# Score products behind the transposes in the dense and the banded attention loops

## The reference

```python
# first block, each layer: swiglu; then a mixer of three branches; then swiglu
y_a = fourier_mix(a_in) @ w_br_a[l]
y_b = dilated_mixture(qb, kb, vb, rel_bias[:, :DIL_HEADS]) @ w_br_b[l]
y_c = diff_attention(qc, kc, vc, ...) @ w_br_c[l]      # the dense loop
merged = gates[:, :, 0] * y_a + gates[:, :, 1] * y_b + gates[:, :, 2] * y_c
# diff_attention: 4 heads, 4 blocks of 128 queries, 512 keys, two maps m
p = jax.nn.softmax(logits, axis=-1)
a = p[:, :, 0] - lam * p[:, :, 1]
o = jnp.einsum('bhqk,bkhe->bqhe', a, vf)
# second block: banded attention with a sink, a gated delta net, cross attention, swiglu
attn_o = _window_attention(aq, ak, av, attn_sink[l])    # the banded loop: keys within 128
```

## Time and profile before

| | before |
|---|---|
| median of three runs | 3817.81 us |
| the profiled execution | 3812.61 us |
| its span | 3810.5 us |
| TensorE products busy | 3582.8 us, 94% |
| TensorE weight loads busy | 2932.3 us, 77% |
| VectorE busy | 1588.3 us, 42% |
| ScalarE busy | 1353.9 us, 36% |
| GpSimd busy | 1480.5 us, 39% |

### The profile page before, as it was taken

How to read it: one execution, slowest core, us unless ns; L and a number is a source line. 1 busy time by engine, 2 the same in 40 slices (tenths; PEclk the granted TensorE clock), 3 DMA queues, 4 the chain that set the end, 5 groups by cost and what they waited for, 6 DMA issues and landing times.

```text
span 3810.5 us, 50432 instructions
## 1 busy us (share of the span) xinstructions
PE 3582.8 (94%) x16768; PEld 2932.3 (77%) x16768; DVE 1588.3 (42%) x2199; ACT 1353.9 (36%) x2332; POOL 1480.5 (39%) x1124
## 2 busy tenths in 40 slices
PE   8999998999999999999989999998888978779997
PEld 6888886778888788878767888886668867558886
DVE  4223225644322422232265442324876675333224
ACT  4224222644322433242346342324571013233223
POOL 4445430345444544454213544443220006225443
PEclk9999998999999999999999999999898989989999
DMA  3223310122222322232112322222110003112222
GB/s 116 94 99 104 117 67 32 63 98 94 95 98 95 105 99 94 99 128 87 46 43 72 105 94 99 94 99 89 50 61 1 1 17 121 50 44 96 97 97 91
DMA packets 86868, 309.59 MB, mean 81 GB/s; under 512 B 9775, under 2 KB 11825, under 8 KB 86244
## 3 DMA queue, kind: packets, MB, share of 16 engines
q1 hardware_dynamic: 82512, 297.96, 23.1%
q10 hardware_dynamic: 4244, 10.14, 1.0%
HBM read 305.89 MB, written 2.17 MB: 81 GB/s over the span
## 4 chain that ended last, share of the span: by engine, by line
PE 89%; DVE 6%; ACT 2%; issue 2%; ACTq 0%; POOL 0%; DMA 0%; DVEq 0%; POOLq 0%
PE ps L416 25%; PE ps L418 25%; PE ps L417 25%; PE ps L814 1%; PE ps L822 1%; PE ps L818 1%; PE ps L563 1%; PE ps L586 1%; PE ps L473 1%; PE ps L453 1%; PE ps L475 1%; PE ps L576 1%; PE ps L501 0%; PE ps L728 0%; PE ps L881 0%
## 5 line engine op out<-in xcount | busy, mean ns | idle before, releaser
L381 POOL TENSOR_TENSOR w_lo<-raw,w_hi 128x512 fp32r<-128x512 f32 x1120 | 1480.3, 1328 | 2301.5 <-ACT w_hi L911 1825.9
L416 PE MATMUL ps<-u_hi,w_hi 128*128 128x512 f32 (+1 forms) x2990 | 1178.3, 394 | 34.2 <-DVE u_lo L1643 16.9
L418 PE MATMUL ps<-u_lo,w_hi 128*128 128x512 f32 (+1 forms) x2990 | 1160.1, 388 | 0.0
L417 PE MATMUL ps<-u_hi,w_lo 128*128 128x512 f32 (+1 forms) x2990 | 1159.8, 388 | 0.0
L416 PEld LDWEIGHTS ps<-u_hi,w_hi 128*128 128x128 f32 x2990 | 569.4, 190 | 165.6 <-issue 41.9
L417 PEld LDWEIGHTS ps<-u_hi,w_lo 128*128 128x128 f32 x2990 | 569.0, 190 | 116.2 <-issue 5.2
L418 PEld LDWEIGHTS ps<-u_lo,w_hi 128*128 128x128 f32 x2990 | 567.8, 190 | 114.7
L913 ACT ACTIVATE w_hi<-raw 128x512 fp32r<-128x512 f32 x560 | 352.5, 629 | 766.5 <-PE ps L418 765.8
L416 PE MATMUL ps<-m_hi,w_hi 128*128 128x512 f32 x1344 | 532.7, 396 | 17.3 <-DVE m_lo L1408 11.9
L911 ACT ACTIVATE w_hi<-raw 128x512 fp32r<-128x512 f32 x560 | 350.9, 627 | 519.6 <-PE ps L418 484.2
L417 PE MATMUL ps<-m_hi,w_lo 128*128 128x512 f32 x1344 | 527.4, 392 | 0.0
(11 more groups left out here) (389 smaller groups left out, 2823.6 us busy)
## 6 DMA issues: line engine op xcount, KB each, us to landing
raw<-jobs SPq DMA_DIRECT2D x560, 512.0 KB, 3.2
tab<-vec_dram ACTq DMA_DIRECT2D x8, 448.0 KB, 5.1
tab<-dft_in ACTq DMA_DIRECT2D x2, 1156.0 KB, 5.2
x<-x_in SPq DMA_DIRECT2D x4, 512.0 KB, 6.5
out<-x SPq DMA_DIRECT2D x8, 256.0 KB, 2.0
tab<-chunk_in ACTq DMA_DIRECT2D x1, 1024.0 KB, 4.8
tab<-mem_in ACTq DMA_DIRECT2D x1, 1024.0 KB, 4.9
tab<-vec_dram ACTq DMA_DIRECT2D x4, 128.0 KB, 7.7
```

The source lines that it names most:

```text
L381: pool.tensor_tensor(w_lo[:, s, w], raw[:, s, w], w_hi[:, s, w].bitcast(F32), ALU.subtract).then_inc(lo_done[s], 1)
L416: pe.matmul(ps[bank][:, 0:n], w_hi[:, s, w], hi[:, k, 0:n], start=k == ks[0], stop=False)
L417: pe.matmul(ps[bank][:, 0:n], w_lo[:, s, w], hi[:, k, 0:n], start=False, stop=False)
L418: last = pe.matmul(ps[bank][:, 0:n], w_hi[:, s, w], lo[:, k, 0:n], start=False, stop=k == ks[-1])
```

## The change

In both loops the call of `scores(u + 2)` moves from the head of the round to the place behind the transposes, ahead of the job. Nothing else is changed.

```diff
@@ dense
                 for u in range(16):
-                    if u < 14:
-                        scores(u + 2)
                     h = 3 - u // 4
                     pe.wait_ge(prob_done, c.next("prob"))
                     pe.wait_ge(tr_copied, c.take("tr_copied"))
                     for k in range(4):
                         mm = pe.transpose(ps[4][:, k * P:k * P + P], T[:, 2 * (u % 2) + 1, k * P:k * P + P], ident)
                     mm.then_inc(tr_full, c.up("tr_full"))
+                    if u < 14:
+                        scores(u + 2)
                     if u % 2 == 0:
                         job(0, u_hi, u_lo)
```

## The result

| | before | after |
|---|---|---|
| median of 7 runs each, same chip | 3817.81 us | 3830.08 us |
| lowest and highest | 3814.16, 3820.9 | 3825.04, 3831.78 |
| the profiled execution | 3812.61 us | 3825.04 us |
| its span | 3810.5 us | 3822.9 us |
| mean granted clock of it | 0.966 | 0.964 |

The ratio is 1.0031, with a 95% interval from 1.0019 to 1.0042: the change costs 12.3 us (7.3 to 16.0 by that interval), more than the 0.2% that a measurement can tell. The forecast of 3818.8 us and its range up to 3824.5 were too low.

What follows compares the result with a forecast made beforehand. TensorE was taken as the bound, with 89% of the chain that ended last. Steady rounds -1.2, dense starts +2.3 and banded start -0.1 summed to +1.0 us, for a median of 3818.8 us, range 3813.0 to 3824.5.

Steps and rivals of the forecast that it cites:

- Steady rounds: 13 rounds in each loop, 39 in all: -0.03 us a round, -1.2 us together, between -5.1 and +3.5.
- Transposes to scores: New pair of starts on TensorE in each steady round, taken as 0.45 us between 0.35 and 0.57.
- First to second product: Start of the job behind the scores in each steady round: 0.33 us, where it was 0.31.
- values to transposes: New pair of starts in each steady round: 0.89 us, read from the last rounds, which have no scores.
- scores to job: New pair of starts in each steady round: 1.06 us, the same as scores to transposes had before.
- Starts: Round 2's scores lose their cover at the dense loop's start, run twice: +2.3 us, between +2.2 and +4.2.
- The banded start: Start of the banded loop, once: transposes go first, job starts earlier; -0.1 us, between -0.3 and +0.1.
- The sum over the loops: Steady rounds plus dense and banded starts: +1.0 us, between -3.2 and +7.8.
- rows 7 and 8: Profile rows of the first dense loop's start: TensorE at 1.2 GHz, clock rise behind 662.2; 1.15 us lost a time.
- A new wait for the probabilities: Rival at the transposes of even rounds: late probabilities cost 12.6 us on top of the 1.0, 3831.4 us; chance 0.07.
- Loads pulled ahead: Rival: the job's first load hides behind the scores, 0.19 us saved in each of 39 rounds, 3811.4 us; chance 0.05.
- Nothing at all: Rival: the edit has no effect, starts not exposed because the clock rises earlier by as much, 3817.8 us; chance 0.08.

Runs made afterwards that it cites:

- banded only: New order in the banded loop alone, dense loops as in the kernel before the change: 3818.84 us against 3806.99, ratio 1.0024.
- rounds 1 to 13 alone: New order in rounds 1 to 13 of each loop, round 0 as before: 3822.90 us against 3806.99; repeated, 3824.07 against 3817.66.

## Why the prediction was wrong

*Steady rounds: the term was mis-sized.* Transposes to scores took 0.53 us, where I took 0.45 between 0.35 and 0.57. The working "load 0.47, less 0.11, plus 0.12" had the right form. The gap behind the last load is 0.17, not the 0.12 of the dilated part, and the load is 0.47, where I had leaned towards the 0.42 of loads behind scores. First to second product took 0.34 for 0.33, values to transposes 0.89 and scores to job 1.06, both as forecast. So a round lost 0.08 us instead of gaining 0.03, near the stated bad end of 0.09: +3.1 us instead of -1.2 (2.8 with the banded rounds as they were measured).

*Starts.* +2.5 us for both dense loops (forecast 2.3) is right. So is its reason: the clock rose 5.0 us behind the transposes against 4.9, and the job began 3.05 us behind them (forecast 2.9). The banded start gave -0.04 where -0.1 was forecast. Its step "transposes can run from 2702.35", 2.35 us behind the scores of round 1, held: they came 2.33 behind. The size was off in the transposes themselves, 1.04 us to the scores at the low clock where 0.75 was allowed. Counted down to the first values, the banded start costs 0.15 us (11.65 for 11.50), just outside the bounds.

*The sum over the loops* is 5.6 us instead of 1.0, inside the bounds of -3.2 to 7.8. This is 4.6 of the 11.3 us that the forecast was off by.

*The step that failed* is larger: 6.7 us. I let the sum end at the loops, and put every later stage at nothing, because its instructions are unchanged. The runs show otherwise: the delta net alone, untouched, goes from 298.5 to 301.3 us, and old-order kernels that only enter it 1.1 or 2.2 us later have 297.4 or 303.7. For the rest of the 6.7 us the profiles show low clock in other stages, and no dose was tried on these. The profile of before had the warning in it. Its span holds some 260 us at the low level of the clock, over a hundred of them behind the banded loop, and the rise that I priced in rows 7 and 8 was treated as a thing of that one place. An edit that shifts all later stages by some us moves each of their falls and rises against their work. With the bounds of the own cost alone, no range reached 3830. The spread that before shows on one chip (3798 to 3823) would have been the better measure of what such a shift can do. None of the signs by which the prediction was to be found wrong came true (waits for the probabilities, rounds outside 7.9 to 8.1 us, a rise more than 1 us late): all of them looked at the loops alone.

*A new wait for the probabilities* did not come. The lead did shrink, to 0.40 us where I had said 0.8 in the worst round: lines 1562 and 1563 both run into GpSimd's product (1.03 and 1.49 us), a collision more than I counted. That leaves 0.40 us between the new order and this rival. Logits start 694.27 - 691.67 = 2.60 us behind the values (forecast 2.57).

*Loads pulled ahead* fell: the job's load stays idle for 0.76 us behind the half-height scores. The Trainium skill's rule on pulling loads ahead (named in the prediction) doesn't show for this load; the rows already said so.

*Nothing at all* fell on both parts, 3.1 and 2.5 us.

## What to carry to other kernels

Moving a step on TensorE changes which kinds of products stand next to each other, and each pair has a start of its own that is paid in every round: list the pairs of both orders before moving a step, and where a pair is priced from two nearby rows, expect the worse. Early work put into a wait at a loop's start is worth about what it takes at full clock if the clock's rise stays in its place: 2.08 us of scores at the low clock (1.13 at the high one) cost 1.22 and 1.35 us when they moved out of the wait. For a kernel bound by TensorE with phases of low clock, an edit of a few microseconds can't be judged by the median alone: set its own cost from starts in the trace beside the difference at equal mean clock, and if the two agree but the median doesn't, add a microsecond or two of useless work elsewhere and see in the trace whether the later stages change length.

## What the runs showed of the hardware

- The length of an untouched stage depends on when it is entered. The delta net took 298.5, 297.4, 303.7 and 298.4 us behind 0, 1.1, 2.2 and 3.5 us of added work, at granted clocks of 0.90, 0.90, 0.88 and 0.90.
- Added work can shorten a later stage by more than it takes: 0.5 us of products cut the delta net by 3.9 us (after) and 4.4 us (banded only).
- The half-height scores leave the next full-height load idle for 0.76 us, in either order. They start 0.17 us behind the last load of the transposes and 0.13 us behind that of the values, together with their own.
- VectorE's operation on one column took 1.03 us and the scaling of a 128x512 tile 1.49 us beside GpSimd's operation with two inputs; away from it the same lines took 0.16 and 0.49 us in before.

What stays open: which of two lengths (143.9 or 150.9 us) the stretch behind the delta net takes, how the 6.7 us divide among the stages over many executions, and why rounds 1 to 13 alone cost 15.9 us on one chip and 6.4 on another.
